# Second mixer: gates, branches and output projection as seven block products

## The reference, cut to what matters

```python
def mixer_out(y, xh, p_rest, n_chunks, ...):
    z, uv, gate_a, gate_b = split_cols(p_rest, [SSD_WIDTH, 2 * MLP_WIDTH, D_MODEL, D_MODEL])
    ssd = ssd_output(y, xh, z, d_skip, ssd_norm_w)          # y * silu(z), normalised over groups of 256
    u, v = jnp.split(jax.nn.gelu(uv), 2, axis=-1)
    sgu = spatial_gating(u, v, n_chunks, ln_w, ln_b, w_s, b_s)
    merged = jax.nn.sigmoid(gate_a) * (ssd @ w_pa) + jax.nn.sigmoid(gate_b) * (sgu @ w_pb)
    return merged @ w_o
...
    h = h + g1_l * mixer_out(...)
```

## Time and profile before

| | us |
|---|---|
| median of three runs | 3599.01 |
| the profiled execution | 3597.85 |
| its span | 3596.1 |
| PE busy | 3360.2 (93%) |
| DVE busy | 1619.2 (45%) |
| ACT busy | 660.8 (18%) |
| mean granted TensorE clock | 0.965 of full speed |

### The profile page before, as it was taken

The page is one execution under the profiler, slowest core; times in us unless marked ns, Lnnn a source line. Parts: engine busy times, 40 slices in busy tenths (PEclk is TensorE's granted clock), DMA queues, the critical chain, the costliest instruction groups (busy, mean ns, idle before and its releaser), DMA issues. The chain is left out here.

```text
span 3596.1 us, 38416 instructions
## 1 busy us (share of the span) xinstructions
PE 3360.2 (93%) x14588; PEld 2306.7 (64%) x14588; DVE 1619.2 (45%) x2312; ACT 660.8 (18%) x1065; POOL 310.2 (9%) x240
## 2 busy tenths in 40 slices
PE   6999987899998999987899997998969999899998
PEld 5888844588887888844488885745744443434342
DVE  4665365466646665456366635343334001311112
ACT  1111015111102111015111102412542000200000
POOL 2110000111100111000111101000320000100000
PEclk8999998999999999998999998899989999999999
DMA  5443221343323443221334321222112332899996
GB/s 132 116 112 95 77 59 30 82 117 91 102 94 82 102 102 100 78 59 36 82 89 115 97 91 32 82 64 76 38 45 71 82 93 91 317 409 410 410 410 272
DMA packets 490114, 453.18 MB, mean 126 GB/s; under 512 B 33994, under 2 KB 438781, under 8 KB 489756
## 3 DMA queue, kind: packets, MB, share of 16 engines
q1 hardware_dynamic: 487920, 449.97, 39.3%
q10 hardware_dynamic: 1452, 1.67, 0.4%
q0 software_dynamic: 640, 0.15, 0.0%
HBM read 445.96 MB, written 5.77 MB: 126 GB/s over the span
## 5 line engine op out<-in xcount | busy, mean ns | idle before, releaser
L457 PE MATMUL psum<-arena 128*128 128x256 f32 x7392 | 1621.8, 381 | 20.3 <-DVE arena L806 20.3
L457 PEld LDWEIGHTS psum<-arena 128*128 128x128 f32 x7392 | 1403.2, 190 | 221.3 <-issue 23.1
L871 DVE TENSOR_TENSOR arena<-arena 128x512 f32<-128x512 f32 (+2 forms) x152 | 97.6, 642 | 608.4 <-PE psum L457 579.5
L2159 PE MATMUL psum<-arena 128*64 128x512 f32 x1536 | 345.8, 600 | 0.8 <-ACT arena L2248 0.8
L354 POOL TENSOR_TENSOR arena<-arena 128x1024 f32<-128x1024 f32 x96 | 180.3, 1900 | 1044.2 <-DVE arena L861 999.3
L695 ACT COPY arena<-psum 128x256 f32<-128x256 f32 x104 | 38.9, 374 | 1182.8 <-PE psum L457 1182.8
L2159 PEld LDWEIGHTS psum<-arena 128*64 128x64 f32 x1536 | 106.8, 137 | 232.6 <-issue 231.6
L1386 PE MATMUL psum<-arena 128*128 128x512 f32 (+1 forms) x576 | 216.9, 537 | 12.7 <-ACT arena L1602 6.4
L1578 PE MATMUL psum<-arena 128*128 128x512 f32 x512 | 220.3, 591 | 0.0
L567 PE MATMUL psum<-arena 128*128 128x512 f32 x416 | 186.3, 606 | 9.8 <-DVE arena L1013 6.2
L1386 PEld LDWEIGHTS psum<-arena 128*128 128x128 f32 x576 | 113.0, 198 | 113.7 <-issue 105.7
(11 more groups left out here) (396 smaller groups left out, 2906.0 us busy)
## 6 DMA issues: line engine op xcount, KB each, us to landing
arena<-in_w_gate_dram SPq DMA_DIRECT2D x64, 1024.0 KB, 14.1
arena<-in_w_up_dram SPq DMA_DIRECT2D x64, 1024.0 KB, 15.1
arena<-in_w_down_dram SPq DMA_DIRECT2D x64, 1024.0 KB, 17.5
arena<-in_ffn_w_gate_dram SPq DMA_DIRECT2D x88, 512.0 KB, 5.9
arena<-in_ffn_w_up_dram SPq DMA_DIRECT2D x88, 512.0 KB, 7.2
arena<-in_ffn_w_down_dram SPq DMA_DIRECT2D x96, 384.0 KB, 3.7
arena<-in_w_in_dram SPq DMA_DIRECT2D x144, 256.0 KB, 3.1
arena<-in_ada_w_dram SPq DMA_DIRECT2D x48, 512.0 KB, 4.0
```

The source lines that it names most:

```text
L457: mm = pe.matmul(psum[:, b0 + b, c:c + HT], w, right(x), start=(first and c == 0), stop=last, skip_group_check=True)
L871: dve.tensor_tensor(sv[:, 0, :, :], a21, a22, ALU.add)
L2159: mm = pe.matmul(psum[64 * e:64 * e + 64, bank0 + half, :], x[:, k, 64 * e:64 * e + 64], ring[u % SLOTS][:, e, half * 512:(half + 1) * 512 ...
```

## The change

- The merge loop and the output projection become 20 joint units, written out one after the other instead of hardware loops. A unit computes 256 output features for 512 tokens. Its weight is 1024 x 256, taken as 2 x 2 blocks of 512 x 128, its right side as 2 x 2 blocks of 512 x 256. Seven block products, each four matmuls of 256 columns, replace eight: 28 matmuls of 256 columns a unit, in a set of four banks (sets alternate). Units 0 to 15 come in four rounds of gate a, gate b, branch a, branch b; units 16 to 19 are the output projection.
- DVE makes the sums of weight blocks for a unit (`weight_sums`, four instructions of 512 columns), two units ahead. Sums of the right-hand side (`right_sums`, one instruction of 512 columns and two of 256, for each of four k) are made once for `xm`, `y`, `sgu` and `merged`, between other work.
- After a unit ACT copies one block (256 columns), and DVE's `collect` adds the products up in SBUF (three instructions of 512 columns, one of 256). Sigmoid, the gate products and the residual's update then work on 1024 columns or two times 512 from SBUF.
- Weights come through three slots of 2048 columns. The third lies over tiles of the scan's beginning. A unit's load (two DMAs of 512 KB) is issued when the unit three before it is done.
- `ws_in` has memory of its own and is loaded at the program's start, ahead of the small weight `w_dt`; its transposes go to banks 2 and 3.
- The first two z weights are loaded ahead of the wait for `y_used`; the load of joint unit 0 comes behind the layer norm's loads and ahead of the other z weights.
- The last `group_var` is done in the middle of joint unit 0.

```diff
-        ws_in = x_flat[:, 0:1024].rearrange("p (g j) -> p g j", g=8)
...
         v_sum, v_var = place(NT), place(NT)
+        ws_in = place(8, 128)
...
+            sp.dma_start(ws_in, d["w_s_2"][0].rearrange("g i j -> i g j")).then_inc(s["ws_in_s"], 16)
             sp.dma_start(w_dt, tiles(d["w_in_2"][0, :, 2048:2080])).then_inc(s["wdt_in"], 16)
...
             single(UB, 2, UC + 512)
+            single(ZP, 1, ZC)
 
             sp.wait_ge(s["y_used"], 16)
...
-            sp.dma_start(ws_in, d["w_s_2"][0].rearrange("g i j -> i g j")).then_inc(s["ws_in_s"], 16)
-            single(ZP, 4, ZC)
-            with sp.Fori(1, 9) as i:
...
+            def joint_load(u, name, c0):
+                if u:
+                    sp.wait_ge(unit_done, JOINT + u)
+                else:
+                    sp.wait_ge(s["xbc_ready"], 12 + 16)
+                to = w_blocks(u).rearrange("p d k f c -> p d k (f c)")
+                for half in range(2):
+                    sp.dma_start(to[:, half, :, :], tiles(d[name][0, 512 * half:512 * half + 512, c0:c0 + 256]))\
+                      .then_inc(joint_in[(u + 2) % 3], 16)
+
+            joint_load(0, "w_in_2", GA)
+            single(ZP + 1, 3, ZC + 256)
+            for u in range(1, 16):
+                name, c0 = KINDS[u % 4]
+                joint_load(u, name, c0 + u // 4 * 256)
             sp.wait_ge(s["mix_used"], 8)
             sp.wait_ge(s["res_out"], 16)
             sp.dma_start(res, d["res_scratch"]).then_inc(s["res_back"], 16)
-            single(WO, 4, 0, "w_o_2")
+            for u in range(16, 20):
+                joint_load(u, "w_o_2", (u - 16) * 256)
...
+            def joint_unit(u, x, x_sum):
+                m = u % 2
+                wv, sv, b0 = w_blocks(u), wsum[m], 4 * m
+                for k in range(4):
+                    if u == 2:
+                        pe.wait_ge(s["y_sums"], k + 1)
+                    if u == 16:
+                        pe.wait_ge(s["merged_sums"], k + 1)
+                    if u == 0 and k == 2:
+                        group_var(3)
...
+                    for b, c, w, xb in ((0, 0, wv[:, 0, k, 0, :], B11), (0, HT, wv[:, 1, k, 0, :], B21),
+                                        (3, 0, sv[:, 2, k, :], B22), (1, 0, sv[:, 1, k, :], T2),
+                                        (1, HT, wv[:, 1, k, 1, :], T4), (2, 0, sv[:, 0, k, :], T1),
+                                        (2, HT, wv[:, 0, k, 1, :], T3)):
+                        mm = pe.matmul(psum[:, b0 + b, c:c + HT], w, right[xb], start=(k == 0 and c == 0),
+                                       stop=(k == 3), skip_group_check=True)
+                mm.then_inc(unit_done, 1)
+
+            for u in range(20):
+                pe.wait_ge(s["sums_ok"], u + 1)
+                if u == 0:
+                    pe.wait_ge(s["xm_sums"], 4)
+                elif u == 1:
+                    pe.wait_ge(s["mix_used"], 8)
+                    pe.wait_ge(s["gstd"], 4)
+                else:
+                    pe.wait_ge(s["collected0" if u % 2 == 0 else "collected1"], u // 2)
+                if u == 3:
+                    pe.wait_ge(s["sgu_sums"], 4)
...
+            for u in range(20):
+                act.wait_ge(unit_done, JOINT + u + 3)
+                act.copy(blocks[u % 4][:, 4, :], psum[:, 4 * (u % 2), 0:HT]).then_inc(s["first_ok"], 1)
+                if u < 16 and u % 4 < 2:
...
+                    act.activation(blocks[u % 4][:, 0:4, :], blocks[u % 4][:, 0:4, :], ACT.Sigmoid)\
+                       .then_inc(s["sig_ok"], 1)
...
             gate_y(0)
+            for k in range(4):
+                right_sums(xm, xm_sum, k, "xm_sums")
             gate_y(1)
...
             gate_y(2)
+            weight_sums(0)
             gate_y(3)
...
+            weight_sums(1)
+            dve.drain()
+            for k in range(2):
+                right_sums(y, y_sum, k, "y_sums")
             norm_y(3)
...
+            for u in range(20):
+                collect(u)
+                if u == 0:
+                    weight_sums(2)
+                    for k in range(2, 4):
+                        right_sums(y, y_sum, k, "y_sums")
+                    for k in range(4):
+                        right_sums(sgu, sgu_sum, k, "sgu_sums")
...
+                    if u % 4 == 3:
...
+                        dve.tensor_tensor(merged[:, 2 * j:2 * j + 2, :].rearrange("p a b -> p (a b)"), other, own,
+                                          ALU.add)
+                        if j >= 2:
+                            dve.drain()
+                            for k in (2 * j - 4, 2 * j - 3):
+                                right_sums(merged, merged_sum, k, "merged_sums")
+                if 0 < u < 18:
+                    weight_sums(u + 2)
```

More of the change, by code:

```diff
@@ L1219, in second_mixer_program, with four_sums @@
         v_sum, v_var = place(NT), place(NT)
+        ws_in = place(8, 128)
+        HT = T // 2
+        wsum = [arena[:, wsum_at + 1536 * i:wsum_at + 1536 * (i + 1)].rearrange("p (s k c) -> p s k c", s=3, c=128)
+                for i in range(2)]
+        blocks = [arena[:, scan_at + 1280 * i:scan_at + 1280 * (i + 1)].rearrange("p (b t) -> p b t", t=HT)
+                  for i in range(4)]
+        assert wsum_at + 3072 <= scan_at and scan_at + 5120 <= mem["size"]
+        def four_sums(flat):
+            return flat.rearrange("p (c k h t) -> p c k h t", c=2, k=4, h=2)
+        xm_sum = four_sums(state[0].rearrange("p a b -> p (a b)"))
+        y_sum = four_sums(arena[:, b_tok_at:b_tok_at + 4096])
+        sgu_sum = four_sums(tail)
+        merged_sum = four_sums(xbc_flat[:, 0:4096])
+        T1, B11, T3, B21, B22, T2, T4 = range(7)
         PN1, PCB, PSN, PCW = 64, 80, 96, 112
@@ L1528, in _ @@
                 for q in range(4):
[L1529 removed]
+                    mm = pe.transpose(psum[:, 2 + r, q * 128:(q + 1) * 128], ws_in[:, 4 * r + q, :], ident)
             mm.then_inc(s["ws_tr"], 1)
@@ L1558, in _ @@
                     mix(2 * (n - 4) + 1)
-            group_var(3)
             pe.wait_ge(bank_free[0], MERGE + 1)
             pe.wait_ge(bank_free[1], MERGE + 1)
[L1562 to L1580, removed]
@@ new lines, in _ @@
+            for u in range(20):
[9 more added lines that the diff above has]
+                    pe.wait_ge(s["sgu_sums"], 4)
+                if u >= 16:
+                    joint_unit(u, merged, merged_sum)
+                else:
+                    joint_unit(u, *((xm, xm_sum), (xm, xm_sum), (y, y_sum), (sgu, sgu_sum))[u % 4])
@@ L1691, in _ @@
             for r in range(2):
-                last = act.copy(ws_T[:, 4 * r:4 * r + 4, :].rearrange("p a b -> p (a b)"), bank(6 + r))
+                last = act.copy(ws_T[:, 4 * r:4 * r + 4, :].rearrange("p a b -> p (a b)"), bank(2 + r))
             last.then_inc(s["ws_ok"], 1)
@@ L1715, in _ @@
             group_std(3)
[L1716 to L1722, removed]
+            for u in range(20):
+                act.wait_ge(unit_done, JOINT + u + 3)
+                act.copy(blocks[u % 4][:, 4, :], psum[:, 4 * (u % 2), 0:HT]).then_inc(s["first_ok"], 1)
+                if u < 16 and u % 4 < 2:
+                    act.wait_ge(s["collected0" if u % 2 == 0 else "collected1"], u // 2 + 1)
+                    act.activation(blocks[u % 4][:, 0:4, :], blocks[u % 4][:, 0:4, :], ACT.Sigmoid)\
+                       .then_inc(s["sig_ok"], 1)
         @block.vector
@@ L1956, in _ @@
                     norm_y(n - 5)
+            weight_sums(1)
+            dve.drain()
+            for k in range(2):
+                right_sums(y, y_sum, k, "y_sums")
             norm_y(3)
[L1958 to L1966, removed]
-                    dve.drain()
-                    dve.tensor_tensor(merged[:, bass.ds(i * 2 + turn, 1), :].rearrange("p a b -> p (a b)"), ga, gb,
-                                      ALU.add).then_inc(bank_free[1], 1)
```

80 lines of the change are left out of this document (63 added, 17 removed).

## The result

The changed kernel takes 3557.76 us (3555.76 to 3558.56, 4 runs) against 3598.74 (3597.97 to 3599.84, 4 runs): a ratio of 0.9885, 95% interval 0.9869 to 0.9900. The forecast was 3558.

The account below looks back on a forecast made before the run. PE, busy for 93% of the span, and its gaps were taken to set the time. 3597.85 - 32.7 - 9.4 + 1.0 + 1.4 - 4.5 + 3.5 = 3557.2, plus 1.2: 3558 us (3555 to 3563, chance 0.60).

Parts of the forecast that it names:

- The products: Merge loop and output projection: 560 matmuls of 256 columns replace 320 of 512, -32.7 us (-34.4 to -29.7).
- The front: Scan's end to first mix: PE's wait for `w_s` goes, new DVE work limits the gain, -9.4 us (-5 to -11.4).
- First units: Joint unit 3: DVE's sums ready just as PE ends unit 2, margin nil, +1.0 us (0 to 4.5).
- Unit 11's turn: Steady state of the joint units: DVE's worst turn, 11.8 us against PE's 12.13, hidden by 0.3.
- Unit 16: Output projection's third k waits for its sums, ready at 7.5 and wanted at 6.1: +1.4 us, no clock fall.
- The seam: Between merge loop and output projection: the 2.56 us gap and the half clock behind it go, -4.5 us.
- The tail: Behind PE's end: ACT's copy, `collect` and two residual instructions take 4.5 us instead of 1.0, +3.5 (2.5 to 5).
- The head: Program's start: `ws_in` loaded ahead of `w_dt` and the first weights, covered by 13 us, 0 (0 to 1).
- front gives most back: v's chain or low clock keeps z units late, front -5; waits at units 3 and 16 grow: 3566 us, chance 0.21.
- margins hold: No wait at unit 3, products at 0.430 us each, front at -11: 3554 us, chance 0.10.
- the half-lost gain: Joint units: block products dearer than in the first block, 0.46 us each, +15: 3573 us, chance 0.05.
- the slower case: PE waits for DVE at every joint unit, with half clock behind each gap: 3648 us, chance 0.02.

Follow-up runs that it names:

- eight_products: Changed kernel with each joint unit's seven block products replaced by 16 plain matmuls of 512 columns, DVE's sums still made and collecting by two copies: 3586.68 us.
- front_alone: Kernel before with only early `ws_in` load in own memory, z weights loaded earlier and transposes in other banks, no block products: 3590.24 us.
- last_plain: Changed kernel with only unit 19 as a plain product into two banks, the residual read straight from them: 3557.31 us.
- dve_heavy: Changed kernel with eleven extra DVE instructions of 512 columns, each with a drain, ahead of the weight sums of units 4 to 19: 3610.51 us.

## Why the prediction was right, point by point

- **The products** (-32.7): right. A step from copy to copy is 12.12 us for 28 products, 0.4329 each, against the forecast's 0.4333. With `group_var`, the wait of 1.36 and the 0.28 at unit 13 off, the 560 take 242.8 us, 0.4336 each, with what the waits cost over their length. The first block's straight-line stretch was the right row; its average over all units would have missed by 3 us. Taken away in *eight_products* the term is 275.05 - 242.8 = 32.2; that the kernel loses only 29.5 by it is the waits (1.6) and the 1.1 of tail that it saves.
- **The front** (-9.4): right in the sum, -9.38. z2 began at 2695.70, which is 2695.0 without the 0.7 by which this trace is late, within the 2694 to 2696 of both bounds. PE waited for both of the things named as late next, Silu for 1.20 and `v_ok` for 0.63. `v_ok` had been put at 2716.2 and came at 2717.15, or 2716.4 without the 0.7; the 0.45 that DVE stood ahead of L2048 with nothing to wait for are more than the difference. A `v_ok` at 2716.2 would have made the front -9.7; the -9.4 was put down without a word on the 0.3 between them, and that it came out to the tenth is luck.
- **First units** (+1.0): did not come. The sums for unit 3 were done at 2787.32 + 0.69 = 2788.0, and unit 2 ended near 2788.3. The margin was 0.3 and not nil, so the +1.0 was an allowance that wasn't needed.
- **Unit 11's turn** ("hidden by 0.3"): failed, by 0.28. DVE stood 0.46 ahead of L2084 there, and unit 13 began that much late (the 12.40 between copies). The turn itself was sized rightly (its terms add up to 11.7, not 11.8); the hold was the thing that it did not include. There were two such holds, of 0.45 and not of one us each, and they cost at most 0.7 us in all. The Trainium skill (Advanced Engine Details and Errata, ISA Cache) gives an engine's instruction memory lines of 256 instructions. The holds here stand at multiples of 128 instructions (last section), so if they are fetches, the pieces are half as large as by that rule. No run here shows that they are fetches.
- **Unit 16** (+1.4): right, a wait of 1.36 with no fall of the clock. It lengthened the unit's step by 1.63; the forecast's own terms add up to 7.4 less 6.1, 1.3.
- **The seam** (-4.5): right. Products behind it run at the full-clock price from the first, and *front_alone*, which has a seam of the old kind, still waits 2.56 there.
- **The tail** (+3.5): right, 4.49 - 1.03 = 3.46 (the forecast's terms add up to 4.4, not 4.5), and *last_plain* shows that it is this chain, by taking it away.
- **The head** (0): right. `w_s` landed 6.2 us after its issue, and from the mixer's first matmul to the scan's end it is 458.24 us, against 458.28 before.
- **The rivals**: "front gives most back" wanted 4.4 of the front and 2 more at each of units 3 and 16, and nothing of it came; "margins hold" had unit 3 right but not the front; the half-lost gain and the slower case did not come, and *dve_heavy* shows what the latter would have needed.

The span fell by 1.3 more than the sum of the terms. Of that, 1.0 is +0.7 ahead of the change and -1.7 in the experts, which no edit made. The other 0.3 are unit 3's +1.0 that didn't come, against +0.3 at unit 13, +0.2 at unit 16 and +0.1 and +0.2 at places thought unmoved. That the median came within 0.3 us of 3558 is luck as well: the four runs lie 2.8 us apart.

## What to carry to other kernels

Price a new instruction from the stretch of the same kernel that runs it under the same conditions (straight-line, no waits), and not from the average or from half of a larger one. When a long wait goes, follow both chains that were hidden under it to their ends: here they took back 2.3 of 11.7 us, and putting one Silu ahead of four squares gave these 2.3 back. Faster products that must be recombined lengthen the tail of the last unit; do that unit plainly when its extra product is cheaper than the recombining.

## What the runs showed of the hardware that was not expected

- **The length of a gap alone didn't settle the clock.** In *dve_heavy* a gap of 2.56 us was followed by a full granted clock and a unit of 12.38 us at 2865.98, and by one of 14.07 at 2989.77; 2.45 was followed by 14.07 and 2.96 by 12.38. The same 2.56 at the seam of the kernel before was followed by 0.50. What decides between them these runs don't show.
- **A low clock costs little while another engine sets the pace.** In *dve_heavy* low-clock units are 1.7 to 3 us longer, and the whole is still within 2 us of what the waits alone were expected to cost.
- **DVE stands for 0.45 us at fixed places of its code.** With the new DVE code every kernel holds 0.45 to 0.46 ahead of the bias addition (L2048 in the changed kernel), with nothing to wait for, and the changed kernel holds 0.46 at L2084 in unit 11; *front_alone*, without that code, has neither. *eight_products* has its second hold at 2810.57 (0.44). In *dve_heavy*, where DVE has work nearly all the time, there are four more, at 2847, 2901, 2952 and 3003. Two of them in its timeline of DVE:

```profile
2847.39 0.69 DVE L2012 TENSOR_TENSOR arena<-arena 128x512 f32<-128x512 f32 x1 [0.43 <-issue]
...
2952.46 5.29 DVE L2012 TENSOR_TENSOR arena<-arena 128x512 f32<-128x512 f32 x7 [0.42 <-issue]
```

  Count DVE's instructions in the kernels' code from the bias addition on, with the drains, and a wait as part of the instruction behind it (two waits in a row make one more). Then every hold stands at a multiple of 128: at 128 in *eight_products*, at 256 in the changed kernel, at 256, 384, 512 and 640 in *dve_heavy*. The way of counting waits was chosen afterwards, but it is one choice for six places. In *dve_heavy* each of the four is followed, 0.7 to 1.0 us behind its end, by one transfer of 8 KB on a DMA queue that the profile marks `instruction` (q14), which has other transfers with no hold near them. That speaks for code that is loaded in blocks of 128 instructions, and against data. It isn't shown: no run moves the block limits alone, and not every multiple has a hold (at 128 in the changed kernel there is none).
